# Residual sums and norms by column halves, norms rounded straight from the banks, two norms folded into one, and modulation slots moved off the FFN ends, in a four-layer model on one core

## What is computed

```python
h = x
h = h + moba_attention(rms_norm(h, norm_mix[0]), ...)      # norm 0
h = h + conv_ffn(rms_norm(h, norm_ffn[0]), ...)            # norm 1, FFN 0
h = h + rwkv7_time_mix(rms_norm(h, norm_mix[1]), ...)      # norm 2
h = h + conv_ffn(rms_norm(h, norm_ffn[1]), ...)            # norm 3, FFN 1
x = rms_norm(h, norm_final)                                # norm 4, over rows
for l in range(2):
    sh1, sc1, g1, sh2, sc2, g2 = split(silu(c) @ ada_w[l] + ada_b[l], 6)   # the modulation
    h = rmsnorm(x, ln1_g[l]) * (1 + sc1) + sh1             # norms 5 and 7
    x = x + g1 * (concat(lru(h), diff_attention(h)) @ w_out[l])
    h = rmsnorm(x, ln2_g[l]) * (1 + sc2) + sh2             # norms 6 and 8
    x = x + g2 * (swiglu(h) if l == 0 else moe(h))         # FFN 2, or router and 8 experts
return rmsnorm(x, final_g)                                 # norm 9
# rms_norm(x, g) = x / sqrt(mean(x * x) + eps) * g
```

## Time and profile before

| | |
|---|---|
| median of 3 runs | 2235.91 us |
| the profiled execution | 2234.21 us, its span 2232.4 us |
| PE matmul busy | 2041.5 us (91%), 12420 instructions |
| DVE busy | 1729.6 us (77%) |
| ACT busy | 1249.3 us (56%) |
| mean granted TensorE clock | 0.95 of full |
| HBM read | 531.47 MB, 239 GB/s over the span |

### The profile page before, as it was taken

How to read it: one execution, slowest core, us unless ns; L and a number is a source line. 1 busy time by engine, 2 the same in 40 slices (tenths; PEclk the granted TensorE clock), 3 DMA queues, 4 the chain that set the end, 5 groups by cost and what they waited for, 6 DMA issues and landing times. The chain is left out here.

```text
span 2232.4 us, 31508 instructions
## 1 busy us (share of the span) xinstructions
PE 2041.5 (91%) x12420; PEld 1783.6 (80%) x12421; DVE 1729.6 (77%) x1962; ACT 1249.3 (56%) x1230; POOL 49.6 (2%) x87
## 2 busy tenths in 40 slices
PE   6999996987799979889988859999999999999995
PEld 5879995977689978789988757888888788888884
DVE  6758786786578877677776757898989898988885
ACT  4654444531344445643334626777777777777773
POOL 0000000000000000000000000000000000000000
PEclk9999998996699999999998979999999999999997
DMA  6347861201366654278872317989999998999893
GB/s 239 133 164 260 298 250 59 95 20 39 118 234 244 248 180 137 109 254 310 294 283 100 114 64 283 369 340 339 354 341 356 334 364 337 369 335 371 333 369 131
DMA packets 79053, 534.07 MB, mean 239 GB/s; under 512 B 11633, under 2 KB 13041, under 8 KB 15201
## 3 DMA queue, kind: packets, MB, share of 16 engines
q1 hardware_dynamic: 71424, 481.04, 57.7%
q0 software_dynamic: 7376, 51.25, 6.2%
q10 hardware_dynamic: 144, 0.26, 0.0%
HBM read 531.47 MB, written 1.05 MB: 239 GB/s over the span
## 5 line engine op out<-in xcount | busy, mean ns | idle before, releaser
L2494 DVE TENSOR_TENSOR weights_lo<-ring,weights_hi 128x2048 fp32r<-128x2048 f32 x288 | 656.4, 2290 | 95.1 <-ACT weights_hi L2488 93.0
L2488 ACT CAST weights_hi<-ring 128x2048 fp32r<-128x2048 f32 x288 | 550.8, 1916 | 157.7 <-PE bank L2637 66.0
L373 DVE TENSOR_TENSOR weights_lo<-ring,weights_hi 128x2048 fp32r<-128x2048 f32 x162 | 370.8, 2291 | 160.1 <-ACT weights_hi L365 158.9
L562 PE MATMUL bank<-acts_hi,weights_hi 128*128 128x256 f32 x1600 | 460.8, 288 | 22.3 <-DVE acts_lo L395 22.3
L365 ACT CAST weights_hi<-ring 128x2048 fp32r<-128x2048 f32 x162 | 308.7, 1907 | 264.7 <-PE bank L562 229.2
L562 PE MATMUL bank<-acts_hi,weights_lo 128*128 128x256 f32 x1600 | 454.6, 284 | 0.0
L562 PE MATMUL bank<-acts_lo,weights_hi 128*128 128x256 f32 x1600 | 453.8, 284 | 0.0
L562 PEld LDWEIGHTS bank<-acts_hi,weights_hi 128*128 128x128 f32 x1600 | 305.7, 191 | 29.6 <-issue 27.1
L2637 PE MATMUL bank<-weights_hi,xg_hi 128*128 128x512 f32 x768 | 307.4, 400 | 5.0 <-DVE xg_lo L2757 3.9
L562 PEld LDWEIGHTS bank<-acts_lo,weights_hi 128*128 128x128 f32 x1600 | 306.2, 191 | 2.7 <-issue 1.4
L562 PEld LDWEIGHTS bank<-acts_hi,weights_lo 128*128 128x128 f32 x1600 | 305.2, 191 | 0.0
(11 more groups left out here) (414 smaller groups left out, 2672.4 us busy)
## 6 DMA issues: line engine op xcount, KB each, us to landing
ring<-in_experts SPq DMA_DIRECT2D x288, 1024.0 KB, 5.4
ring<-in_dense SPq DMA_DIRECT2D x162, 1024.0 KB, 4.8
ada<-in_ada POOLq DMA_DIRECT2D x48, 1024.0 KB, 5.1
silu_c<-in_c SPq DMA_DIRECT2D x3, 512.0 KB, 3.7
resid<-in_x SPq DMA_DIRECT2D x1, 1024.0 KB, 6.7
out<-resid SPq DMA_DIRECT2D x1, 1024.0 KB, 4.0
cst<-in_consts SPq DMA_DIRECT2D x1, 649.5 KB, 9.0
kh<-in_rwkv_g SPq DMA_DIRECT2D x1, 512.0 KB, 9.1
```

The costliest lines, as they stand in the source:

```text
L373: nc.vector.tensor_tensor(split[1][:, n % SPLITS, :], ring[:, n % RING, :], split[0][:, n % SPLITS, :].bitcast(F32), ALU.subtract).then_in ...
L562: ins = nc.tensor.matmul(bank[:, f * T:(f + 1) * T], split[w][:, m % SPLITS, k * 256 + f * P:k * 256 + (f + 1) * P], acts[x][:, k, :], sta ...
L2488: nc.scalar.copy(split[0][:, (moe_first + j) % SPLITS, :], ring[:, slot, :]).then_inc(hi_ready, 1)
L2494: nc.vector.tensor_tensor(split[1][:, at, :], ring[:, (moe_first + j) % RING, :], split[0][:, at, :].bitcast(F32), ALU.subtract).then_inc( ...
```

## The change

1. `project` orders the last block by bank: both tiles and both column halves in turn, 6 matmuls each, with a signal after each of the first three banks. Before, one signal came after 12 of the 24.
2. `add_projected` waits for each bank by itself, and `summed` counts halves. The norm's second tile is squared, multiplied and transposed by halves.
3. Ahead of the sums, DVE splits one block less (`after + 1`), at FFN ends two less (`last + 1`); they come after the columns of the norm. ACT rounds one block less ahead of the norm at FFN ends.
4. A norm without shift (norms 0, 1 and 3) is rounded straight from the bank: ACT writes `acts_hi`, DVE computes bank times gain minus `acts_hi`.
5. Norms 4 and 5 are one (`TwoNorms`): the second root comes from the sum of squares of `resid * norm_final`, taken before the first root is known. `resid` itself is written afterwards.
6. The slot (j, 1) of the last FFN step is gone. FFN 0 keeps 13 pieces, FFN 1 has 13 for 12, FFN 2 has 22 for 23.
7. The rope angles of the second model's positions move from DVE's first instructions into step 1 of the first attention. Norm 0 splits one weight block ahead, not three.
8. The router joins the joint block; its DMA is issued when the last sum is done. The split of the first three expert blocks on DVE moves from the router to behind `Sel`. The last norm is in the block of the last sum, works tile by tile and stores each tile by its own DMA.

The core of the diff:

```diff
-            slots = sorted([(j, 1) for j in range(pairs)] + [(j, 0) for j in twice])
+            slots = sorted([(j, 1) for j in range(pairs - 1)] + [(j, 0) for j in twice])
...
-        plan_ffn(2, [(1, i) for i in range(1, 24)], range(1, 12))
+        plan_ffn(2, [(1, i) for i in range(2, 24)], range(1, 12))
...
             def act_columns(self, act):
-                for b in range(2):
+                for b in range(4 if self.direct else 2):
                     act.wait_ge(turned, 4 * self.turns + b + 1)
...
+                        dst = acts[0] if self.direct else AT
+                        ins = nc.scalar.activation(dst[:, f, :], pb[b][:, i * T:(i + 1) * T], ACT.Identity,
                                                    scale=self.gain(f), bias=self.bias(f) if self.bias else 0.0)
...
             def dve_columns(self, dve):
...
                     for c in range(4):
-                        at_rest(dve, self.no, c)
+                        if self.direct:
+                            dve.wait_ge(at_hi, 4 * self.no + c + 1)
+                            for i in range(2):
+                                f = 2 * c + i
+                                ins = nc.vector.scalar_tensor_tensor(acts[1][:, f, :], pb[c][:, i * T:(i + 1) * T], self.gain(f),
+                                                                     acts[0][:, f, :].bitcast(F32), ALU.mult, ALU.subtract)
+                            ins.then_inc(at_lo, 1)
+                        else:
+                            at_rest(dve, self.no, c)
                 if self.then is not None:
                     rest_to(dve, self.then + self.look)
...
+        class TwoNorms(Norm):
...
+            def added(self, dve, t, h):
+                w = self.halves[t][h]
+                if t + h == 0:
+                    dve.wait_ge(gain_in, 16)
+                dve.wait_ge(summed, self.sums + 2 * t + h + 1)
+                nc.vector.tensor_tensor(xn[:, t, w], resid[:, t, w], self.final[:, w], ALU.mult).then_inc(normed, 1)
...
+            if last:
+                steps = [(f, t, x, w, h) for t in range(TT) for h in range(2) for f in range(2) for x, w in PARTS]
+            else:
+                steps = [(f, t, x, w, h) for f in range(2) for t in range(TT) for x, w in PARTS for h in range(2)]
...
+                if last and n in (5, 11, 17):
                     ins.then_inc(half_done, 1)
...
-                        rest_to(dve, at["down", pairs - 1] + 4)
+                        rest_to(dve, last + 1)
...
-                        add_projected(dve, last, scale, zz, joined=joined or norm is not None)
-                        if norm is not None:
-                            norm.dve(dve)
+                        add_projected(dve, last, scale, zz, then=norm)
+                        norm.dve(dve)
...
+                    sp.wait_ge(summed, sums[0])
                     sp.dma_start(router[:], a["moe_router_2"][0].rearrange("(k p) n -> p k n", p=P)).then_inc(late_in, 16)
...
-                    for j in range(SPLITS):
-                        moe_lo(dve, 0, j)
                     dve.wait_ge(r_exp, 1)
```

More of the change, by code:

```diff
@@ L403, in build @@
         PARTS = ((0, 0), (0, 1), (1, 0))
[L406 to L436, removed]
@@ L449, in __init__, with begin @@
                 self.no = new_split() if parts else None
                 self.joined = joined
+                self.halves = [[slice(0, D)] if t == 0 or not joined else [slice(0, D // 2), slice(D // 2, D)] for t in range(TT)]
                 self.sums = sums[0]
                 if joined:
-                    sums[0] += TT
+                    sums[0] += 2 * TT
+                self.begin()
+            def begin(self):
+                self.squares, self.rooted, self.normed = squares_made[0], roots_made[0], normed_made[0]
+                squares_made[0] += sum(3 if len(h) > 1 else 1 for h in self.halves)
+                roots_made[0] += TT
+                normed_made[0] += sum(len(h) for h in self.halves)
@@ L597, in project @@
+            for n, (f, t, x, w, h) in enumerate(steps):
+                ins = nc.tensor.matmul(pb[4 + 2 * t + h][:], src[x][:, tile + f, t * P:(t + 1) * P],
+                                       split[w][:, m % SPLITS, f * D + h * 512:f * D + (h + 1) * 512],
+                                       start=(c == 0 and f == 0 and w + x == 0),
+                                       stop=(last and f == 1 and x == 1))
+                if last and n in (5, 11, 17):
                     ins.then_inc(half_done, 1)
@@ L630, in finish @@
-        def finish():
-            stored = sem("stored")
-            with engine_programs() as block:
-                @block.sync
-                def _(sp):
-                    sp.dma_start(out[0].rearrange("(t p) d -> p t d", p=P), resid[:]).then_inc(stored, 16)
-                    sp.wait_ge(stored, 16)
+                    nc.vector.tensor_tensor(r, r, y, ALU.add).then_inc(summed, 1)
+                    added[0] += 1
+                    n += 1
+                    if then is not None:
+                        then.added(dve, t, h)
@@ L1067, in ffn @@
             last = at["down", pairs - 1] + 1
-            ahead(then + (2 if norm is None else norm.look))
+            ahead(then + norm.look)
             with ExitStack() as stage:
@@ L2503, in _ @@
                 def _(pool):
+                    pool.wait_ge(summed, sums[0])
                     pool.memset(yacc[:], 0.0).then_inc(m_y, 4)
@@ L2877, in _ @@
                     select(dve, 0, 0, False)
+                    for j in range(SPLITS):
+                        moe_lo(dve, 0, j)
                     keep_gate(dve, 0, None)
```

334 lines of the change are left out of this document (210 added, 124 removed).

## The result

The changed kernel takes 2208.19 us (median of 4 runs, 2202.96 to 2214.38); in the same comparison the kernel before takes 2235.26 us (2232.08 to 2238.18). The ratio is 0.9885, with a 95% interval of 0.9861 to 0.9909. The profiled execution took 2206.66 us, its span is 2204.8 us. The kernel is faster, by 27 us where 37 were forecast; the time lies inside the range and 2 us above the likeliest case's own.

A forecast was written before the change was run, and what follows sets the result against it. PE was taken as the bound, multiplying for 91% of the span; gains in its gaps summed to 37.1 us, from 2234.21 to 2197.1, predicted median 2198 us. Range 2188 to 2211; the likeliest case (0.52) had 2192 to 2206.

The forecast's parts named there:

- The gaps at the stage ends: PE's wait before a norm's transpositions: 1.8 us without a gate, 2.4 with one, 6.5 after FFN 1.
- attention and RWKV end: Shorter gaps there gain 0.7 us each; the split moved behind the norm might lose 0 to 1 us.
- Rival A: Covers fail: moved splits late for PE's second block, 1 us at each of 6 norms, other losses; 2210 us, chance 0.22.
- FFN 0 to RWKV: At FFN 0's end 6.4 us gained, 4.6 back from two splits before `xn<-AT`, which starts some 1.8 us earlier.
- FFN 2: Without its last slot, no 7.36 us wait, lower-clock window or extra matmul, and a shorter gap: 11.2 us gained.
- One slot more in FFN 1: DVE's 2.6 us there mostly covered by PE: 0.5 us lost, bounds 0 and 2.6.
- Rounding from the bank: Norms 1 and 3: first matmul 4.2 us after the first transposition, 1.5 us per norm, 3.0 us gained.
- rival B: Shorter gaps keep the clock up in transpositions and the router, 9 us more gained; 2189 us, chance 0.20.
- C: Slower: clock grants fall the other way, 1.8 us per half-clock window, 25 more windows; 2243 us, chance 0.03.
- D: No change: the experts' weight stream, not PE, sets the end; about 2235 us, chance 0.03.
- Two norms in one: After FFN 1, transpositions start from 828.5 against 833.00: 4.5 us gained, bounds 2 and 7.
- The start: Angles moved and norm 0 not waiting for three splits: first matmul near 19.4 us, 2.0 us gained, bounds 0.5 and 5.5.

The follow-up runs named there:

- run 3: run 2 with GpSimd's memset of `yacc` moved from mixer 1's last sum to behind mixer 1's norm; 2193.73 us, ratio 0.9792.
- run 1: The changed kernel again, nothing edited; 2210.80 us, ratio 0.9866 to the kernel before.
- run 2: The changed kernel with SP issuing fewer weight blocks ahead, so `silu_c` goes out early, in four places; 2195.94 us, ratio 0.9804.
- Run 8: The changed kernel with only DVE's two splits ahead of `xn<-AT` moved behind the RWKV stage's LoRA work; 2202.01 us, ratio 0.9843.
- run 10: run 9 with the three FFNs' modulation slots as in the kernel before the change; 2181.57 us, ratio 0.9770.
- run 9: run 3 with RWKV splits behind the LoRA work, angles parted around norm 0's rows, second constants piece behind one weight block; 2177.61 us, ratio 0.9760.
- run 7: The changed kernel with the rope angles at DVE's start again, ahead of the first norm; 2204.89 us, ratio 0.9859.

## Why the prediction was right, and where its sum was off

The direction and the places were right: PE's idle time ahead of the norms was what the change took away. (It was the largest single share of PE's idle time, 50.7 of 191 us, and not most of it, as I wrote.) That the time lies in the forecast's range is in part luck: a loss of 15 us that was not in the sum stood against gains of the clock that the sum did not count either. Step by step:

- **The gaps at the stage ends** are within 0.4 us of the forecast at six of seven places, so the account of bank by bank (one bank's work, a reciprocal, one multiplication) holds. At the seventh, mixer 1, a wait that was not in the sum took 1.6 us: the memset had also been released by the last sum (run 3).
- **The step that failed** is the one on attention and RWKV end: of the split that goes behind the norm I wrote that it "is then late if PE is through its first new block (5.7 us) before it ends", and took PE as the only one who waits for it. PE did not. SP did, through the ring place, with `silu_c` behind it, then ACT and the third block. That cost 11.9 us in waits in the first profile, 14.1 in run 1's, and 14.9 us of time by runs 1 and 2. Rival A priced the moved splits at 6 us, before the second block; run 2 rules out that mechanism, since the split ends as late there and PE has no gap. Its 2210 us were nearer to the time than the forecast's 2198 by luck.
- **FFN 0 to RWKV**: the forecast laid the two splits in front of `xn<-AT` and let 4.6 us come back. Run 8 measured 4.3. But from FFN 0's last matmul to `xn<-AT` it is 354.73 - 345.26 = 9.5 us, where it was 356.08 - 342.91 = 13.2: 3.7 us gained and not 1.8, since the 16 transpositions took 1.94 us here too, for 3.65 before (351.13 to 354.78).
- **FFN 2**: 11.2 us forecast and, without the late `silu_c`, 13.8 measured for a stretch where 12.1 were forecast. The whole was about right and its division wrong. I put the 7.36 us down to the slot; 4.0 of it were the split ahead of it (run 10).
- **One slot more in FFN 1**: 0.5 us of loss forecast. FFN 1's stretch is 200.2 us in run 9's profile and 198.3 with the slots as before (run 10's), so it was 1.9, within the bounds; the shorter gap at FFN 1's end gave 0.8 of it back.
- **Rounding from the bank**: 3.0 us forecast, 1.9 seen in the gaps. DVE's new instruction took 0.475 us (24 in the trace), where I took 0.45. The estimate of 0.39 from the table in the Trainium skill (VectorE: DVE Perf Modes, The TRN2 errata) is further off; the measurement decides. PE's first matmul came 3.3 us after the first transposition where I had 4.2: the 16 transpositions took 2.04 us at the full clock, and had taken 3.62 us at about half. The first window is the kernel before, the second the one after (columns as above; the granted clock is the last but two):

```profile
147.78:151.40 3.62, 3.61 (x16) 3.27 (x16) 1.26 (x3) 1.51 (x6) 0.59 (x2) 0.53 0.82 326
```

```profile
144.37:146.40 2.03, 2.03 (x16) 1.71 (x16) 1.05 (x3) 0.78 (x3) 0.59 (x2) 1.00 0.47 105
```

  So rival B's mechanism was there too, and about in its size. First to last transposition, the seven norms took 24.7 us before and 17.6 after, and the router's 32 matmuls 6.97 and 5.11: 9.0 us together, where B had 9 (not all of it reaches the time). It is not steady: behind the gap of 3.98 us the transpositions took 3.44 us here and 2.45 to 3.57 in the other runs with that gap. And it goes the other way too (mixer 0, the experts' entry). C was wrong in its price as well (10 matmuls for 2.3 us of work in 3.50 are 1.2 us, not 1.8). C and D had no share: the granted clock over the span was 0.95 before and is 0.956 now, and the experts passed on all but 0.9 us of what was gained ahead of them.
- **Two norms in one**: 10.99 to 6.38 us, 4.6 us for 4.5 forecast. But the stretch gained only 3.0: behind this norm PE's matmuls began at half clock, where they had begun at the full one, and 1.6 us went there. PE's first 3 us of blocks, before and after (us, PE busy with its matmuls, granted clock, DMA share, GB/s):

```profile
838.94:841.94 3.00, 3.00 (x25) 1.00 0.02 5
```

```profile
835.85:838.85 3.00, 3.00 (x14) 0.50 0.02 5
```

- **The router's DMA**: PE starts 1.57 us after the last transposition, as forecast. **The experts' entry**: 5.7 us and not 2.7. Up to the gather 7.0 were gained for 5.2, of which 1.9 are the router's faster matmuls; and only 1.3 came back for 2.5, since DVE's splits were done 0.1 us after PE's gather, which took 6.43 us (granted clock 0.58) where I had counted 5.2. **The end**: 5.5 us for 4.5.
- **The start**: 2.6 us for 2.0, with the first matmul at 19.10 us for 19.4. But I counted the angles' move among its causes; run 7 shows that it cost 3 us and gave none, since the constants set the first matmul either way.

## What to carry to other kernels

When work is moved in one engine's program, list everything that waits for its result, the DMA queue above all: a queue that waits for a buffer to come free holds up all that stands behind it, also small transfers which have nothing to do with the buffer. Such a shift is seen in no comparison of the instruction orders, only in who waits for whom. A stall can also hide what other edits are worth: undoing the rounding from the banks cost no time that could be measured while `silu_c` was late; in the traces it lost the same 1.9 us of PE's time with and without that wait.

## What the runs showed of the hardware

- A multiplication on DVE (128x1024, float32, 0.75 us elsewhere) took 2.36 us beside a memset on GpSimd of 1.80 us that began within 0.02 us of it, and 0.75 us again when the memset was moved (run 3). The DVE instruction ended 0.54 us after the memset, whose own length did not change. The Trainium skill (SBUF — State Buffer, Who interferes with whom) says that a `tensor_scalar` on VectorE can use a pair of ports that it shares with GpSimd, that the one which issues first holds it for its whole instruction, and that the other is blocked. The length and the end of the DVE instruction agree with that; the order doesn't show, since by the trace the blocked one began 0.02 us ahead.
- A 512 KB transfer (`silu_c`) took 3.6 to 4.0 us from issue to landing when SP issued it 2.6 us or more behind a block of 1 MB (kernel before), and 5.6 to 7.1 us when it was 0.4 us behind one (kernel after).
